# Two projection seams without a wait for the last stores, loads moved into the projections' tails, and a PSUM copy shared with ScalarE

## The chip, the cores and the metric

The kernel runs on one core of a Trainium2 chip. The metric is the device time of one execution, in microseconds. Three runs of the kernel before gave 2546.37, 2546.48 and 2543.38 us (median 2546.37). TensorE (PE) does matmuls and transposes into PSUM, VectorE (DVE) and ScalarE (ACT) do element-wise work and read PSUM, GpSimd (POOL) does element-wise work in SBUF and issues some DMAs, SyncE (SP) issues most DMAs.

## The reference, cut to what matters

A two-layer encoder on 2048 tokens of width 1024, all in float32:

```
h = rms_norm(x, g0); u = h @ w_in_even                   # 2048 x 3328
a = diff_attention(aq, ak, av)       # 4 heads, two maps each, causal by chunks of 64
b = swa_sink_attention(bq, bk, bv)   # 8 heads, window of 128 keys, sinks
x = x + concat(a * silu(ag), b * silu(bg)) @ w_out_even
h = rms_norm(x, g1); u = h @ w_in_odd                    # 2048 x 4096
c = chunk_attention(cq, ck, cv)      # 16 heads, a chunk sees itself and 8 before
x = x + (c * silu(cg)) @ w_out_odd
return rms_norm(x, final_g)
```

## The kernel before, in words

Six stages run one after the other. Each is a block with one program per engine, and between two blocks all five engines meet in a barrier: a stage begins when the last engine has come to the end of its program. In the trace the stages begin about here: first projection 0 us, differential attention 609.0, small (window) attention 978.6, first output 1076.7, second projection 1288, chunk ("band") attention 1964.4, second output 2348.0.

**The projections** (`project`) multiply by one level of Strassen: seven products for a pair of column blocks (a slab, numbered `e`), each of 12 matmuls of 128x128 by 128x512 (high and low parts, L1092). Two passes over the tokens with 13 slabs (first projection) or 16 (second) make `G` slabs; each gives four blocks of 128x512, numbered `n`. The last slab's four blocks are gate blocks in both projections. A gate block goes this way: DVE adds up the products in `full_out` (L945 to L978), ACT makes the sigmoid in `lo_out` (L592), DVE multiplies it into `hi_out` (L868), SP stores it to the DRAM tensor `gt` in two DMAs (L487). `lo_out` and `hi_out` have two buffers each; before ACT writes block `n` it waits until the store of block `n - 2` has landed. At the end SP waits until all stores have landed, and only then does it come to the barrier (L527).

In the last slab POOL already loads operands of the next attention from the DRAM tensors `qh` and `ql` into SBUF that held operands of products that are done (`FirstAhead`, `BandAhead`; POOL waits for the number of finished products, `mm_done`). In the first projection these are the keys of the first 512 tokens after two products, and the queries after six. In the second they are the first 768 columns of four tensors of queries and keys, after four products (L1173). PE waits for them at its first matmul of the attention (`ahead.loaded`).

**The differential attention** begins with 13 DMAs by SP for each further block of 512 tokens, and a small load of the bias by ACT (L1489).

**The band attention** (`band_attn`) goes in 128 steps (8 pairs of heads, 16 token tiles). In each PE makes logits for two heads (L1800), DVE adds the bias and takes the maximum (L1867), ACT exponentiates (L1896), PE turns the result (L1821), DVE and ACT copy it to SBUF, PE multiplies by the values (L1844). PE's logits of step `s + 1` wait for the maxima of step `s`. At the stage's start SP and ACT issue the loads of the columns not yet there and of the values (L1681 to L1685), and POOL loads and masks the bias for the first two heads (L1740 to L1750), then for the next two; DVE's first maximum waits for the first of these (`bias_set`).

**The small attention** (`small_attn`) goes in 32 steps of two tiles and two heads. By step `n`: PE logits (L2043), DVE four maxima into `prob` (L2094), ACT four exponentials (L2130), PE 16 transposes of 64x64 into `turned` (L2057), which lies in two PSUM banks and exists once, DVE one copy of both banks to `prob_t` (L2103), PE the product with the values (L2070). The programs run staggered: PE does logits of step `n`, transposes of `n - 1`, products of `n - 2`; DVE the maxima of `n`, then the copy of `n - 1`. The transposes of a step wait for the copy of the step before. ACT copies the output after every second step (L2137).

## Time and profile before

| what | value |
|---|---|
| runs | 2546.37, 2546.48, 2543.38 us, median 2546.37 |
| profiled execution | 2548.01 us, of which its span is 2546.2 us |
| PE busy | 2369.5 us, 93% of the span |
| DVE, ACT, POOL busy | 1531.6 (60%), 1137.0 (45%), 1071.1 us (42%) |
| mean granted clock of PE | 0.976 of full speed |

The profile lists idle time of an engine with what ended it: another engine, a DMA, or "PEq" where it was PE's own sequencer that came to the instruction late, as it does behind a barrier. PEclk is the clock that was granted to PE, 1.00 for 2.4 GHz and 0.50 for 1.2 GHz.

### The profile page before, as it was taken

Reading aid. Unit: us, or ns where it says so; the run is one execution under the profiler, and the core shown is the slowest. Engines: PE = TensorE matmul, PEld = TensorE weight load, DVE = VectorE, ACT = ScalarE, POOL = GpSimd, SP = SyncE. Lnnn points to the kernel's source line nnn. Section 1 sums busy time; section 2 is a strip of 40 time slices with the busy share of each in tenths; the row PEclk is TensorE's granted clock in tenths of the full one; section 3 lists DMA queues with packets and bytes.
Section 4 is the critical chain, followed back from the end, with each engine's and each line's share of the span. In section 5 each row is a group of like instructions: output and inputs, shape, how many; then the busy total and the mean of one; then the engine's idle time right before and its main releaser. Section 6 shows DMA issues by size and latency. Waiting matters only on the chain. (4 is left out here: it accounts for less than half of the span.)

```text
span 2546.2 us, 46284 instructions
## 1 busy us (share of the span) xinstructions
PE 2369.5 (93%) x17864; PEld 1973.5 (78%) x17864; DVE 1531.6 (60%) x2862; ACT 1137.0 (45%) x2403; POOL 1071.1 (42%) x852
## 2 busy tenths in 40 slices
PE   5999999997999998899879999899997999998998
PEld 4777778875888887688768888788886888887887
DVE  6444565334988897966554423744223888888555
ACT  4333343333777776612143333433332666665221
POOL 6687758773000002310068877678774201100100
PEclk9999999997999999999989999999998999999999
DMA  3555434466663243757334444344433463454452
GB/s 125 173 182 174 157 114 146 145 190 148 138 146 76 62 129 106 219 211 277 130 125 167 157 118 140 116 150 164 141 100 116 159 199 131 148 174 117 163 201 83
DMA packets 220745, 376.76 MB, mean 148 GB/s; under 512 B 54980, under 2 KB 108912, under 8 KB 219504
## 3 DMA queue, kind: packets, MB, share of 16 engines
q1 hardware_dynamic: 199376, 296.21, 36.6%
q0 software_dynamic: 19792, 75.50, 10.0%
q8 instruction: 144, 2.36, 0.4%
q10 hardware_dynamic: 1360, 2.10, 0.3%
q14 instruction: 73, 0.60, 0.1%
HBM read 236.33 MB, written 142.90 MB: 149 GB/s over the span
## 5 line engine op out<-in xcount | busy, mean ns | idle before, releaser
L1092 PE MATMUL p_acc<-p_operands,p_w_hi 128*128 128x512 f32 x1600 | 611.7, 393 | 5.8 <-DVE p_full_out L959 5.5
L310 POOL TENSOR_TENSOR p_w_lo<-p_w_raw,p_w_hi 128x512 fp32r<-128x512 f32 x240 | 333.1, 1396 | 151.3 <-ACT p_w_hi L573 151.0
L1092 PE MATMUL p_acc<-share,p_w_hi 128*128 128x512 f32 x1024 | 385.0, 396 | 12.0 <-DVE p_operands L735 5.6
L1092 PEld LDWEIGHTS p_acc<-p_operands,p_w_hi 128*128 128x128 f32 x1600 | 302.7, 190 | 67.7 <-POOL p_w_raw L328 4.7
L1092 PE MATMUL p_acc<-share,p_w_lo 128*128 128x512 f32 x896 | 350.8, 392 | 0.0
L573 ACT ACTIVATE p_w_hi<-p_w_raw 128x512 fp32r<-128x512 f32 x252 | 156.5, 624 | 245.4 <-POOL p_w_raw L328 106.5
L1092 PE MATMUL p_acc<-share_low,p_w_hi 128*128 128x512 f32 x624 | 249.3, 400 | 12.1 <-DVE p_operands L735 6.1
L1092 PE MATMUL p_acc<-share_low,p_w_lo 128*128 128x512 f32 x624 | 245.2, 393 | 0.0
L1092 PEld LDWEIGHTS p_acc<-share,p_w_hi 128*128 128x128 f32 x1024 | 192.5, 189 | 54.0 <-DVE p_operands L735 8.5
L865 DVE SCALAR_TENSOR_TENSOR p_lo_out<-p_full_out,p_hi_out 128x512 fp32r<-128x512 f32 x116 | 122.5, 1056 | 182.3 <-ACT p_hi_out L590 182.3
L1867 DVE CUSTOM_DVE_ANT_0 c_prob<-c_logits,c_bias 128x640 f32<-128x640 f32 (+4 forms) x256 | 179.5, 739 | 65.6 <-PE c_logits L1800 49.5
L1896 ACT ACTIVATE c_prob<-c_prob,c_neg_max 128x640 f32<-128x640 f32 (+4 forms) x256 | 193.2, 756 | 43.3 <-DVE c_neg_max L1867 43.3
L2354 PE MATMUL o_acc<-w_out_hi,o_m_hi 128*128 128x512 f32 x512 | 203.2, 397 | 3.3 <-DVE o_m_lo L2289 3.3
L2354 PE MATMUL o_acc<-w_out_lo,o_m_hi 128*128 128x512 f32 x512 | 200.9, 392 | 0.0
L2354 PE MATMUL o_acc<-w_out_hi,o_m_lo 128*128 128x512 f32 x512 | 200.7, 392 | 0.0
L1092 PEld LDWEIGHTS p_acc<-share,p_w_lo 128*128 128x128 f32 x896 | 168.7, 188 | 36.0
L1464 ACT ACTIVATE a_prob<-a_prob,a_neg_max 128x128 f32<-128x128 f32 (+15 forms) x128 | 153.5, 1199 | 64.0 <-DVE a_neg_max L1421 63.6
L310 POOL TENSOR_TENSOR p_w_lo<-ready_w,p_w_hi 128x512 fp32r<-128x512 f32 x96 | 132.2, 1385 | 111.5 <-ACT p_w_hi L573 111.5
L1800 PE MATMUL c_logits<-share 64*128 64x256 f32 (+2 forms) x1440 | 138.1, 322 | 30.0 <-DVE c_neg_max L1867 21.4
L945 DVE COPY p_full_out<-p_acc 128x512 f32<-128x512 f32 x56 | 38.7, 691 | 191.8 <-PE p_acc L1092 191.8
L1800 PEld LDWEIGHTS c_logits<-share 64*128 64x128 f32 x1440 | 111.9, 188 | 54.2 <-DVE c_neg_max L1867 38.5
L1844 PE MATMUL c_o<-c_prob_t,c_v 128*64 128x128 f32 x2240 | 151.5, 279 | 0.4 <-issue 0.3
(284 smaller groups left out, 4743.6 us busy)
## 6 DMA issues: line engine op xcount, KB each, us to landing
scr_qh<-p_hi_out SPq DMA_DIRECT2D x116, 256.0 KB, 2.5
scr_ql<-p_lo_out SPq DMA_DIRECT2D x116, 256.0 KB, 2.7
p_w_raw<-in_w_in_even POOLq DMA_DIRECT2D x26, 1024.0 KB, 7.5
scr_gt<-p_hi_out SPq DMA_DIRECT2D x128, 128.0 KB, 2.0
ready_w<-in_w_in_odd POOLq DMA_DIRECT2D x16, 1024.0 KB, 6.9
p_w_raw<-in_w_in_odd POOLq DMA_DIRECT2D x16, 1024.0 KB, 7.0
share<-scr_qh SPq DMA_DIRECT2D x28, 512.0 KB, 8.1
share<-scr_ql SPq DMA_DIRECT2D x28, 512.0 KB, 9.5
```

The lines of the kernel that those rows point to most:

```text
L310: nc.gpsimd.tensor_tensor(w_lo[:, k, :, :], w_source(e, k), w_hi[:, k, :, :].bitcast(F32), ALU.subtract).then_inc(w_made, 1)
L573: nc.scalar.activation(w_hi[:, k, :, :], w_source(e, k), ACT.Copy).then_inc(w_cast, 1)
L865: nc.vector.scalar_tensor_tensor(out=lo_out[:, buf, :], in0=full_out[:, buf, :], scalar=factor, in1=hi_out[:, buf, :].bitcast(F32), op0=AL ...
L945: nc.vector.tensor_copy(full_out[:, n % 2, :], x[:, :]).then_inc(taken, 1)
L1092: last = nc.tensor.matmul(bank[:, :], wt[:, k, c, :], at[k][:, c, :], start=starts and step == 0, stop=step == 3 * HK - 1, skip_group_chec ...
L1464: nc.scalar.activation(p, p, ACT.Exp, bias=neg_max[:, j:j + 1], scale=-1.0, accum_out=row_sum[:, g % 2, m:m + 1]).then_inc(exp_done, 1)
L1800: last = nc.tensor.matmul(logits[half][:, lo:hi], q_sb[b][x][rows, i * P:(i + 1) * P], k_sb[b][y][rows, tile * P:tile * P + hi - lo], star ...
L1844: last = nc.tensor.matmul(o_ps[half * HD:(half + 1) * HD, at:at + P], v, prob_t[:, s % 2, t, half, :], start=t == 0, stop=t == w - 1)
L1867: nc.vector.tensor_tensor_reduce(out=prob[:, j, 0:n], in0=logits[half][:, END - n:END], in1=bias[:, b, WIDE - n:WIDE], scale=1.0, scalar=H ...
L1896: nc.scalar.activation(p, p, ACT.Exp, bias=neg_max[:, j:j + 1], scale=-1.0, accum_out=sums[:, 2 * hp + half, i:i + 1]).then_inc(exp_done, 1)
L2354: last = nc.tensor.matmul(acc[u % 4][:, :], mt[:, t % 2, c, :], wt[:, c, half * BLK:(half + 1) * BLK], start=step == 0, stop=step == 3 * K ...
```

## The change

It has three parts. The code is of the changed kernel where a line has a plus.

**Gates in place.** The last slab's four gate blocks each have a place of their own (`final_place`: two in `lo_out`, two in `hi_out`): ACT writes the sigmoid there, DVE multiplies in place, SP stores it in one DMA that counts on `gates_stored`. ACT's waits for the stores of the last slab itself are gone, and SP's wait at the end covers the slabs before the last only. Those who write to this SBUF in the next stage, or read the gates, wait for `gates_stored`; to make them few, tensors were moved so that only late ones lie there (in the band attention `o_out` and `w_raw`, in the differential attention the small attention's bias).

**Loads in the tail.** Each query of the first projection is loaded as soon as the product that used its place is done (after 3, 4, 5 and 6 products, two DMAs of 128 KB each). In the second projection the four tensors of queries and keys are loaded to half of their columns after 1, 2, 3 and 4 products, then the other half (`rest`); the bias for four heads is loaded after one product into `ahead_place` (which also holds the projection's `x` and `g` buffers) and masked by POOL before the barrier. The band attention's own start is left with the loads of the values, on SP.

**Shared copy.** In the small attention, after every odd step, DVE copies one bank of `turned` and ACT the other; ACT does so between its second and third exponential of the following step.

```diff
...
@@ -123,6 +123,8 @@
+        hi_out = st.sb("hi_out", [P, 2, HT], F32R)
+        lo_out = st.sb("lo_out", [P, 2, HT], F32R)
@@ -281,6 +281,12 @@
+        FINAL = 4 * G - 4
+        def final_place(n):
+            return (lo_out, hi_out)[(n - FINAL) // 2][:, n % 2, :].bitcast(F32)
@@ -411,10 +417,11 @@
-                pool.wait_ge(sem, 16 * 2 * N)
+                pool.wait_ge(sem, 16 * 2 * (N + ahead.BLOCKS))
+            ahead.set_bias(pool)
@@ -482,6 +489,9 @@
+                    if n >= FINAL:
+                        sp.dma_start(gt[at:at + P, first:first + HT], final_place(n)).then_inc(ahead.gates_stored, 16)
+                        return
@@ -524,7 +534,7 @@
-                sp.wait_ge(sem, 16 * 2 * G)
+                sp.wait_ge(sem, 16 * 2 * (G - 1))
@@ -578,7 +588,12 @@
-                if n >= 2:
+                if n >= FINAL + 2:
+                    act.wait_ge(stored_a[buf], 16 * 2 * (G - 1))
+                    act.wait_ge(stored_b[buf], 16 * 2 * (G - 1))
+                elif n >= FINAL:
+                    act.wait_ge(dve_done, seconds[n - 1])
+                elif n >= 2:
@@ -589,7 +604,8 @@
-                    nc.scalar.activation(lo_out[:, buf, :].bitcast(F32), full_out[:, buf, :], ACT.Sigmoid).then_inc(act_done, 1)
+                    to = final_place(n) if n >= FINAL else lo_out[:, buf, :].bitcast(F32)
+                    nc.scalar.activation(to, full_out[:, buf, :], ACT.Sigmoid).then_inc(act_done, 1)
@@ -864,6 +880,8 @@
+                elif n >= FINAL:
+                    nc.vector.tensor_tensor(final_place(n), full_out[:, buf, :], final_place(n), ALU.mult).then_inc(dve_done, 1)
@@ -1132,48 +1150,83 @@
-    def queries(self, eng):
-        for part, near, far in (("qh", slice(0, HD), slice(HD, P)), ("ql", slice(HD, P), slice(0, HD))):
-            self.load(eng, part, 0, near, slice(2, 6, 2))
-            self.load(eng, part, 0, far, slice(3, 6, 2))
+    def query(self, slot):
+        m, s = divmod(slot - 2, 2)
+        rows = (slice(0, HD), slice(HD, P))
+        def load(eng):
+            for x, part in enumerate(("qh", "ql")):
+                row = m * HD
+                eng.dma_start(self.low[rows[(x + s) % 2], slot, 0:BLK].bitcast(F32), self.scr[part][row:row + HD, 0:BLK]).then_inc(self.loaded, 16)
+        return load
-        return [(2, self.keys), (6, self.queries)]
+        return [(2, self.keys)] + [(slot + 1, self.query(slot)) for slot in range(2, 6)]
-    COLS = 3 * NEAR
+    COLS = SEQ // 2
+    BLOCKS = 2 * C_HEADS * HD // SLAB
+    FAR, SET = 3 * P, 3
-    def both(self, eng):
-        for x, part in enumerate(("qh", "ql")):
-            for slot, row in ((x, 0), (2 + x, C_W)):
-                eng.dma_start(self.whole[:, slot, 0:self.COLS].bitcast(F32), self.scr[part][row:row + P, 0:self.COLS]).then_inc(self.loaded, 16)
+        self.place = ctx.enter_context(nc.sbuf_tensor("ahead_place", [P, 3 * D], F32))
+        self.bias = self.place[:, 0:4 * (self.FAR + NEAR)].rearrange("p (h j) -> p h j", h=4)
+    def load_bias(self, pool):
+        pool.dma_start(self.bias[:, :, self.FAR:self.FAR + NEAR], skewed(self.scr["skew_c"], 0, 4)).then_inc(self.bias_loaded, 16)
+    def set_bias(self, pool):
+        nc, bias = self.nc, self.bias
+        nc.gpsimd.memset(bias[:, :, 0:self.FAR], 0.0).then_inc(self.bias_set, 1)
+        pool.wait_ge(self.bias_set, 1)
+        nc.gpsimd.memset(bias[HD:P, :, 0:HD], MASKED).then_inc(self.bias_set, 1)
+        pool.wait_ge(self.bias_loaded, 16)
+        nc.gpsimd.memset(bias[0:HD, :, self.FAR + NEAR - HD:self.FAR + NEAR], MASKED).then_inc(self.bias_set, 1)
+        pool.wait_ge(self.bias_set, self.SET)
+    def one(self, eng, slot, cols, loaded):
+        row = C_W * (slot // 2)
+        eng.dma_start(self.whole[:, slot, cols].bitcast(F32), self.scr[("qh", "ql")[slot % 2]][row:row + P, cols]).then_inc(loaded, 16)
+    def first(self, slot):
+        return lambda eng: self.one(eng, slot, slice(0, self.COLS), self.loaded)
+    def rest(self, eng):
+        for slot in range(4):
+            self.one(eng, slot, slice(self.COLS, SEQ), self.rest_loaded)
-        return [(4, self.both)]
+        return [(1, self.load_bias)] + [(slot + 1, self.first(slot)) for slot in range(4)] + [(4, self.rest)]
...
@@ -1302,6 +1356,7 @@
+            pool.wait_ge(ahead.gates_stored, ahead.GATES)
...
@@ -1621,14 +1676,16 @@
+        o_out = st.sb("o_out", [P, 2, BLK])
-        bias = st.sb("bias", [P, 4, WIDE])
+        bias = ahead.bias
-        o_out = st.sb("o_out", [P, 2, BLK])
...
@@ -1721,40 +1770,25 @@
-            load_bias(0)
-            mask(nc.gpsimd.memset(bias[:, 0:2, 0:WIDE - NEAR], 0.0))
-            mask(nc.gpsimd.memset(bias[HD:P, 0:2, 0:HD], MASKED))
-            finish_bias(0)
-            load_bias(1)
-            mask(nc.gpsimd.memset(bias[:, 2:4, 0:WIDE - NEAR], 0.0))
-            mask(nc.gpsimd.memset(bias[HD:P, 2:4, 0:HD], MASKED))
-            finish_bias(1)
+            pool.wait_ge(first_loaded[-1], 16)
+            pool.wait_ge(ahead.gates_stored, ahead.GATES)
...
@@ -1785,7 +1819,7 @@
-                        pe.wait_ge(first_loaded[-1], 16 * (LOADS + 1))
+                        pe.wait_ge(ahead.rest_loaded, ahead.LOADED)
@@ -1858,8 +1892,10 @@
-                if i == 0 and half == 0:
-                    dve.wait_ge(bias_set, hp + 1)
+                if s == 0 and half == 0:
+                    dve.wait_ge(ahead.bias_set, ahead.SET)
+                if hp >= 2 and i == 0 and half == 0:
+                    dve.wait_ge(bias_set, hp - 1)
@@ -1898,6 +1934,8 @@
+                if n == 0:
+                    act.wait_ge(ahead.gates_stored, ahead.GATES)
@@ -1909,8 +1947,6 @@
-            for n in range(len(FIRST)):
-                first_piece(act, n, 1)
...
@@ -1970,6 +2006,10 @@
+        def shared(n):
+            return n % 2 == 1
@@ -2047,6 +2087,8 @@
+                    if n // 2:
+                        pe.wait_ge(far_copied, n // 2)
@@ -2060,6 +2102,8 @@
+                if shared(n):
+                    pe.wait_ge(far_copied, n // 2 + 1)
@@ -2099,6 +2143,9 @@
+                if shared(n):
+                    nc.vector.tensor_copy(prob_t[:, n % 2, :, 0:HD], turned[:, 0, :].rearrange("p (x q) -> p x q", q=HD)).then_inc(copied, 1)
+                    return
@@ -2120,9 +2167,17 @@
+            def far_leaves(n):
+                act.wait_ge(turned_done, n + 1)
+                if n >= 2:
+                    act.wait_ge(pv_done, n - 1)
+                nc.scalar.activation(prob_t[:, n % 2, :, HD:P], turned[:, 1, :].rearrange("p (x q) -> p x q", q=HD), ACT.Copy).then_inc(far_copied, 1)
+                    if j == 1 and n >= 1 and shared(n - 1):
+                        far_leaves(n - 1)
@@ -2140,6 +2195,7 @@
+                    far_leaves(N - 1)
...
@@ -2304,6 +2360,9 @@
+                if t == 0:
+                    for sem in post.stored:
+                        dve.wait_ge(sem, 16 * (post.heads // 2))
```

The end of SP's program in the first projection, and the beginning of the next stage; before:

```order
246 L487 DMA scr_gt<-p_hi_out 128x256 [waits p0_dve_done]
247 L487 DMA scr_gt<-p_hi_out 128x256
248 L120 UNCONDITIONAL_BRANCH [waits p0_stored_b1,p0_stored_b0,p0_rows_spread,p0_stored_a1,p0_stored_a0]
249 L1264 UNCONDITIONAL_BRANCH [waits barrier_Pool_Activation_PE_DVE_SP_release]
250 L1260 DMA share_low<-scr_qh 64x512
```

and in the changed kernel:

```order
239 L497 DMA scr_gt<-p_hi_out 128x256
240 L493 DMA scr_gt<-p_lo_out 128x512 [waits p0_dve_done] x2
241 L493 DMA scr_gt<-p_hi_out 128x512 [waits p0_dve_done] x2
242 L120 UNCONDITIONAL_BRANCH [waits p0_stored_b1,p0_stored_b0,p0_rows_spread,p0_stored_a1,p0_stored_a0]
243 L1317 UNCONDITIONAL_BRANCH [waits barrier_Pool_Activation_PE_DVE_SP_release]
244 L1313 DMA share_low<-scr_qh 64x512
```

The last four blocks leave in four DMAs of 128x512 instead of eight of 128x256. The wait at the end names the same semaphores, but its count is that of the slab before.

The end of POOL's program in the second projection (up to the branch L120) and its first instructions in the band attention; before:

```order
691 L1173 DMA share<-scr_qh 128x768 [waits p0_rows_stored,p0_rows_spread,p1_mm_done,p0_ident_set,p0_rows_set]
692 L1173 DMA share<-scr_qh 128x768
693 L1173 DMA share<-scr_ql 128x768 x2
694 L120 UNCONDITIONAL_BRANCH
695 L1726 UNCONDITIONAL_BRANCH [waits barrier_Pool_Activation_PE_DVE_SP_gather]
696 L1740 DMA c_bias<-scr_skew_c 128x2x256
697 L1749 MEMSET c_bias 128x2x384
698 L1750 MEMSET c_bias 64x2x64 [waits p0_x_turned]
699 L1745 MEMSET c_bias 64x2x64 [waits p0_split,p0_x_turned]
```

and in the changed kernel (names of semaphores that stages use in turn are those of the first; the last four loads are `rest`):

```order
696 L1206 DMA ahead_place<-scr_skew_c 128x4x256 [waits p0_v_turned,p0_stored_a0,p0_rows_set,p0_stored_a1,p0_stored_b0]
697 L1219 DMA share<-scr_qh 128x1024 [waits p0_rows_set]
698 L1219 DMA share<-scr_ql 128x1024 [waits p0_rows_set]
699 L1219 DMA share<-scr_qh 128x1024 [waits p0_rows_set]
700 L1219 DMA share<-scr_ql 128x1024 [waits p0_rows_set]
701 L1219 DMA share<-scr_qh 128x1024 [waits p0_rows_set]
702 L1219 DMA share<-scr_ql 128x1024
703 L1219 DMA share<-scr_qh 128x1024
704 L1219 DMA share<-scr_ql 128x1024
705 L1210 MEMSET ahead_place 128x4x384
706 L1212 MEMSET ahead_place 64x4x64 [waits ahead_bias_set]
707 L1214 MEMSET ahead_place 64x4x64 [waits ahead_bias_loaded]
```

The bias's load and three memsets have moved from behind the barrier to ahead of it, and eight loads of 512 KB stand where four of 384 KB stood.

ACT in the first steps of the small attention; before:

```order
655 L2121 UNCONDITIONAL_BRANCH [waits barrier_Pool_Activation_PE_DVE_SP_release]
656 L2130 ACTIVATE b_prob,post_sums<-b_prob,b_neg_max 128x128 [waits b_max_done] x2
657 L2130 ACTIVATE b_prob,post_sums<-b_prob,b_neg_max 128x256 [waits b_max_done] x14
658 L2137 ACTIVATE b_o_out<-b_o 128x512 [waits b_pv_done]
659 L2130 ACTIVATE b_prob,post_sums<-b_prob,b_neg_max 128x256 [waits b_max_done] x8
```

and in the changed kernel:

```order
655 L2185 ACTIVATE b_prob,post_sums<-b_prob,b_neg_max 128x128 [waits b_max_done] x2
656 L2185 ACTIVATE b_prob,post_sums<-b_prob,b_neg_max 128x256 [waits b_max_done] x8
657 L2174 ACTIVATE b_prob_t<-b_turned 128x8x64 [waits b_turned_done]
658 L2185 ACTIVATE b_prob,post_sums<-b_prob,b_neg_max 128x256 [waits b_max_done] x6
659 L2192 ACTIVATE b_o_out<-b_o 128x512 [waits b_pv_done]
660 L2185 ACTIVATE b_prob,post_sums<-b_prob,b_neg_max 128x256 [waits b_max_done] x2
661 L2174 ACTIVATE b_prob_t<-b_turned 128x8x64 [waits b_pv_done,b_turned_done]
```

A copy of 128x512 stands between exponentials once in eight of them, that is once in two steps.

## Rows read from the trace of the kernel before

**Rows 1.** Waits of PE over the span: who for whom, us, times, longest.

```profile
PE c_logits L1800 <- DVE c_neg_max L1867: 21.4, 26, 8.1
...
PE a_logits L1325 <- PEq L120: 9.2, 1, 9.2
...
PE c_logits L1800 <- PEq L120: 8.6, 1, 8.6
...
PE a_logits L1325 <- DMA ready_v<-scr_v_a: 5.9, 1, 5.9
```

**Rows 2.** Timeline, first seam: start, duration, engine, line, tiles [idle before, releaser].

```profile
597.43 7.44 SPq L487 DMA_DIRECT2D scr_gt<-p_hi_out  x6
...
599.89 0.69 DVE L978 TENSOR_TENSOR p_full_out<-p_acc,p_near_sum 128x512 f32<-128x512 f32 x1 [0.41 <-PE p_acc L1092]
602.70 0.63 ACT L592 ACTIVATE p_lo_out<-p_full_out 128x512 f32<-128x512 f32 x1 [3.94 <-DMA scr_gt<-p_hi_out]
603.36 0.69 DVE L868 TENSOR_TENSOR p_hi_out<-p_full_out,p_lo_out 128x512 f32<-128x512 f32 x1 [2.78 <-ACT p_lo_out L592]
...
609.04 1.09 PE L1325 MATMUL a_logits<-share_low 128*128 128x128 f32 x4 [9.19 <-PEq L120]
```

**Rows 3.** Waits of SP's queue over the span.

```profile
SPq L527 <- DMA scr_gt<-p_hi_out: 5.1, 2, 3.5
```

**Rows 4.** DMAs issued from 599.4 to 600.0: KB each, us from issue to landing.

```profile
share_low<-scr_ql POOLq DMA_DIRECT2D x1, 256.0 KB, 8.1
```

**Rows 5.** Timeline, second seam.

```profile
1955.46 0.39 PE L1092 MATMUL p_acc<-share,p_w_lo 128*128 128x512 f32 x1
1958.07 0.63 ACT L592 ACTIVATE p_lo_out<-p_full_out 128x512 f32<-128x512 f32 x1 [5.39 <-DMA scr_gt<-p_hi_out]
...
1960.80 0.69 DVE L868 TENSOR_TENSOR p_hi_out<-p_full_out,p_lo_out 128x512 f32<-128x512 f32 x1 [0.78 <-ACT p_lo_out L592]
...
1964.42 0.91 PE L1800 MATMUL c_logits<-share 64*128 64x128 f32 x6 [8.57 <-PEq L120]
...
1965.32 1.28 ACT L1896 ACT_TABLE_LOAD   x1 [4.55 <-PEq L120]
...
1972.59 0.20 POOL L1745 MEMSET c_bias<- 64x128 f32 x1 [6.05 <-DMA c_bias<-scr_skew_c]
1972.82 0.29 DVE L1867 CUSTOM_DVE_ANT_0 c_prob<-c_logits,c_bias 128x128 f32<-128x128 f32 x1 [11.32 <-POOL c_bias L1745]
...
1973.38 0.58 PE L1800 MATMUL c_logits<-share 64*128 64x256 f32 x2 [8.06 <-DVE c_neg_max L1867]
```

**Rows 6.** DMAs issued from 1964.3 to 1964.5: KB each, us from issue to landing.

```profile
c_v<-scr_v SPq DMA_DIRECT2D x1, 128.0 KB, 5.0
```

**Rows 7.** Stretches: busy us (instructions) of PE, PEld, DVE, ACT, POOL; PEclk, DMA share, GB/s.

```profile
1949.00:1956.00 7.00, 6.85 (x31) 5.33 (x29) 3.37 (x5) 0.80 (x2) 1.46 (x3) 1.00 0.87 238
1958.00:1960.00 2.00, 0.00 (x0) 0.00 (x0) 1.27 (x2) 0.63 (x1) 0.00 (x0) 0.55 0.00 0
1982.00:1984.00 2.00, 2.00 (x40) 1.86 (x36) 1.12 (x4) 0.32 (x3) 0.90 (x1) 0.98 1.03 400
```

**Rows 8.** Groups in the small attention, 980 to 1068: busy us, mean ns | idle before.

```profile
L2137 ACT ACTIVATE b_o_out<-b_o 128x512 f32<-128x512 f32 x15 | 8.6, 574 | 0.0
...
L2103 DVE COPY b_prob_t<-b_turned 128x512 f32<-128x512 f32 x4 | 2.7, 683 | 0.0
```

**Rows 9.** Timeline, two steps of the small attention.

```profile
995.76 0.71 PE L2057 MATMUL b_turned<-keep_ident,b_prob 64*128 64x64 f32 x16
...
997.43 0.98 PE L2043 MATMUL b_logits<-share_low 64*128 64x256 f32 x12
...
998.45 0.48 DVE L2094 CUSTOM_DVE_ANT_0 b_prob<-b_logits,ready_bias,keep_sink 128x256 f32<-128x256 f32 x1
...
1000.07 1.22 DVE L2103 COPY b_prob_t<-b_turned 128x1024 f32<-128x1024 f32 x1
...
1001.34 0.71 PE L2057 MATMUL b_turned<-keep_ident,b_prob 64*128 64x64 f32 x16
```

More of the change, by code:

```diff
@@ L140, in project @@
         XS = 4
-        x_sb = st.sb("x", [P, XS if ready is None else 2, D])
+        x_sb = st.sb("x", [P, XS, D]) if ready is None else ahead.place[:, 0:2 * D].rearrange("p (b d) -> p b d", b=2)
         x_buf = [x_sb[:, i, :] for i in range(XS)] if ready is None else [ready.x[:, 0, :], ready.x[:, 1, :], x_sb[:, 0, :], x_sb[:, 1, :]]
-        g_sb = st.sb("g", [P, D])
+        g_sb = st.sb("g", [P, D]) if ready is None else ahead.place[:, 2 * D:3 * D]
         if norm:
@@ L1131 @@
 class FirstAhead:
-    LOADED = 16 * 6
+    LOADED = 16 * 10
+    BLOCKS = 0
     SPARED = 16 * 12
+    GATES = 16 * 4
     def __init__(self, nc, ctx, scr, low):
         self.scr, self.low = scr, low
-        self.loaded = ctx.enter_context(nc.semaphore("first_ahead"))
+        self.loaded, self.gates_stored = (ctx.enter_context(nc.semaphore(f"first_{x}")) for x in ("ahead", "gates_stored"))
     def load(self, eng, part, row, rows, slots):
@@ L1156, in loads @@
     def loads(self):
-        return [(2, self.keys), (6, self.queries)]
+        return [(2, self.keys)] + [(slot + 1, self.query(slot)) for slot in range(2, 6)]
 class BandAhead:
-    COLS = 3 * NEAR
+    COLS = SEQ // 2
     LOADED = 16 * 4
+    BLOCKS = 2 * C_HEADS * HD // SLAB
+    GATES = 16 * 4
+    FAR, SET = 3 * P, 3
     def __init__(self, nc, ctx, scr, whole):
-        self.scr, self.whole = scr, whole
-        self.loaded = ctx.enter_context(nc.semaphore("band_ahead"))
-    def both(self, eng):
-        for x, part in enumerate(("qh", "ql")):
-            for slot, row in ((x, 0), (2 + x, C_W)):
-                eng.dma_start(self.whole[:, slot, 0:self.COLS].bitcast(F32), self.scr[part][row:row + P, 0:self.COLS]).then_inc(self.loaded, 16)
+        self.nc, self.scr, self.whole = nc, scr, whole
+        self.place = ctx.enter_context(nc.sbuf_tensor("ahead_place", [P, 3 * D], F32))
+        self.bias = self.place[:, 0:4 * (self.FAR + NEAR)].rearrange("p (h j) -> p h j", h=4)
+        self.bias_loaded, self.bias_set = (ctx.enter_context(nc.semaphore(f"ahead_{x}")) for x in ("bias_loaded", "bias_set"))
+        self.loaded, self.rest_loaded, self.gates_stored = (ctx.enter_context(nc.semaphore(f"band_{x}")) for x in ("ahead", "rest", "gates_stored"))
@@ L1287, in _ @@
                     sp.wait_ge(pv_done, TILES * (h + 1))
+                    sp.wait_ge(ahead.gates_stored, ahead.GATES)
                     after.load(sp)
@@ L1515, in __init__ @@
         self.nc, self.keep, self.scr, self.share = nc, keep, scr, share
+        self.bias = ctx.enter_context(nc.sbuf_tensor("ready_bias", [P, B_HEADS, NEAR], F32))
         self.v_flat = ctx.enter_context(nc.sbuf_tensor("ready_v", [P, SEQ], F32))
         self.v_sb = self.v_flat[:, :].rearrange("p (h t d) -> p h t d", h=2, d=HD)
-        self.bias = ctx.enter_context(nc.sbuf_tensor("ready_bias", [P, B_HEADS, NEAR], F32))
         self.loaded, self.keys_loaded, self.bias_loaded, self.masked = (
@@ L1645, in band_attn @@
         bias_loaded = st.sems("bias_loaded", 2)
-        bias_masked, bias_set = (st.sem(x) for x in ("bias_masked", "bias_set"))
+        bias_set = st.sem("bias_set")
         qk_done, max_done, exp_done, pv_done, o_done = (
@@ L1675, in values, with first_values @@
             return v_dram[2 * hp:2 * hp + 2].rearrange("h p t d -> p h t d")[:, :, tiles, :]
-        def first_piece(eng, n, x):
-            cols = slice(*FIRST[n])
-            part = scr[("qh", "ql")[x]]
-            if FIRST[n][1] > ahead.COLS:
-                eng.dma_start(q_sb[0][x][:, cols].bitcast(F32), part[q_row:q_row + P, cols]).then_inc(first_loaded[n], 16)
-                eng.dma_start(k_sb[0][x][:, cols].bitcast(F32), part[k_row:k_row + P, cols]).then_inc(first_loaded[n], 16)
-            if x == 0:
-                tiles = slice(FIRST[n][0] // P, FIRST[n][1] // P)
-                eng.dma_start(v_sb[:, 0, :, tiles, :], values(0, tiles)).then_inc(first_loaded[n], 16)
+        def first_values(eng, n):
+            tiles = slice(FIRST[n][0] // P, FIRST[n][1] // P)
+            eng.dma_start(v_sb[:, 0, :, tiles, :], values(0, tiles)).then_inc(first_loaded[n], 16)
         def load_qk(eng, hp, n):
@@ L1723, in _ @@
                         sp.wait_ge(qk_done, TILES * hp)
+                        sp.wait_ge(ahead.gates_stored, ahead.GATES)
                         post.load(sp)
@@ L1834, in pv @@
                     pe.wait_ge(v_loaded[hp % 2][i // (TILES // HALVES)], 16 * loads(hp))
-                if hp == 0 and i < ahead.COLS // P:
+                if hp == 0:
                     for n, (lo, hi) in enumerate(FIRST):
@@ L1951, in small_attn @@
         pair_loaded = [st.sems(f"pair_loaded{b}_", HALVES) for b in range(2)]
-        qk_done, max_done, exp_done, turned_done, copied, pv_done, o_done = (
-            st.sem(x) for x in ("qk_done", "max_done", "exp_done", "turned_done", "copied", "pv_done", "o_done"))
+        qk_done, max_done, exp_done, turned_done, copied, far_copied, pv_done, o_done = (
+            st.sem(x) for x in ("qk_done", "max_done", "exp_done", "turned_done", "copied", "far_copied", "pv_done", "o_done"))
         sink_less, sink_done, summed = (st.sem(x) for x in ("sink_less", "sink_done", "summed"))
```

29 lines of the change are left out of this document (11 added, 18 removed).

## The prediction

> **What bounds the kernel now.** I read the table of busy time first. PE is busy for 93% of the span, so a change that takes no work off PE can only win time in which PE is idle. The view of waits says where that is [rows 1]: apart from many short waits there are two stops behind a barrier (9.2 us ahead of the differential attention, 8.6 ahead of the band attention), and the longest single wait for the maxima of the band attention, 8.1 us, which turns out to be the second half of the same seam. The reader is to see that these come to 26 us and that all three are at places that the change touches.
>
> The timeline of the two seams says what ends last in each. At the first seam [rows 2] DVE has the last block's sum at 599.89 + 0.69 = 600.58, but ACT's sigmoid begins at 602.70, released by the landing of a store of two blocks earlier. DVE's product ends at 604.05, SP has issued the last two stores at 597.43 + 7.44 = 604.87, and waits 3.5 us for them [rows 3]. PE begins at 609.04, 0.65 us after that. At the second seam [rows 5] the last matmul ends at 1955.85. The sigmoid that starts at 1958.07 is of the last block but one; it again waited for a store. The last product ends at 1961.49 and PE begins at 1964.42. It then makes six matmuls and stops until 1973.38: the first maximum needs the bias, and POOL can finish the bias only at 1972.59, after its DMA. In the small attention PE does not stand still for long; there I look at the chain of steps [rows 9].
>
> **The change, part by part.** First seam. ACT no longer waits for a store: sigmoid about 0.1 after the sum, 600.7 to 601.3 (0.63 long), product 601.35 to 602.05 (0.69). SP issues one DMA instead of two; two took 604.87 - 604.05 = 0.8, so one 0.4: 602.45. It does not wait for the landing, and 0.65 us for the barrier gives a start of PE at 603.1. That is 5.9 us earlier. What must be there by then are the queries. Before, 1 MB of them was issued after six products, and the last DMA took 8.1 us to land [rows 4], until about 607.7, hidden under the wait for the stores. Now only 256 KB are issued so late, the rest one, two and three products earlier. If the last two still took 8.1 us from an issue at 598.6, they would land at 606.7 and take 3.6 of the 5.9 back; a DMA that shares the engines with a quarter of the bytes should take well under half of that, so I take nothing for it and keep 3.6 as the bound. The next stage's 13 loads, for which PE waited 5.9 us [rows 1], now start while the last gate store is under way: I take off 0.5. First seam: **5.4 us** (2.3 to 6.5).
>
> Second seam. Both waits for stores go. The last sum can start 0.04 after the last matmul, as it does at the first seam: 1955.9 to 1956.6. Sigmoid to 1957.3, product to 1958.05, one store issued by 1958.45, barrier: PE begins at 1959.1, 5.3 us earlier. The bias is loaded and masked before, so DVE's first maximum follows PE's six matmuls (0.91 us); from there to PE's next logits it took 1973.38 - 1972.82 = 0.56. The second logits then begin at 1959.1 + 0.91 + 0.05 + 0.56 = 1960.6 instead of 1973.38: **12.8 us** in all. The table load of ACT (1.28) starts at the barrier and ends at 1960.4, about when the first exponential needs it. After this the steps are the same.
>
> What could be late here. POOL must be through with its program before the barrier. A product has 12 matmuls, and PE does 31 in 6.85 us [rows 7], so a product takes 2.65 us and the first one of the last slab ends six products before 1955.85, at 1940. From there 0.5 MB of bias and 2 MB of first halves are needed by 1959.1, and the same stretch of the trace moved 238 GB/s: 2.5 MB and two stores of 256 KB take 12.6 us, until 1952.6. With the 2 MB of second halves it is 1961; those are needed only at the ninth step. Should POOL's issue of a load be held up until the bytes before it have moved, it would come to its memsets near 1959, and the seam would give back about 2. The values are now the first DMA of SP in the stage; before, they landed after 5.0 us [rows 6] among the other loads, and 1959.1 + 5 is about when the first step needs them. I take 12.8, with 9 to 15 as bounds.
>
> On this collision the rows show that the store that ACT waited for at the second seam was slow while POOL's loads ran [rows 5, 7]. The Trainium skill (DMA: Bandwidth & Descriptors, section Issuing engines are not separate DMA queues) says that DMAs from ScalarE, SyncE and GpSimd end up on the same 16 engines and interleave. The trace agrees. By that rule 4.5 MB in the tail slow its stores and each other: as long as nobody waits for a late one the sum stays, and if somebody does, the time is that of the second rival below, 2533.3.
>
> Small attention. DVE's copy of 128x512 takes 0.68 where the whole takes 1.22 [rows 8, 9], so 16 steps save DVE 0.54 each, 8.6 us together; that is the upper bound. I take nearly none of it. From transposes to the transposes two steps later it is 5.58 us [rows 9]: transposes, values and logits of PE from 995.76 to 998.41, DVE's four maxima from 998.45 to 1000.07, the copy until 1001.29, and again transposes at 1001.34. The copy in this chain is that of the step between. Where the transposes are of an odd step it is the copy of an even one, which stays whole, so this chain keeps its 5.58 us for two steps; only the other one gets shorter, by 0.54, and there ACT's own copy of 0.57 [rows 8] stands ahead of two of four exponentials. So DVE and PE change one wait for another. The last step is odd and ends 0.54 earlier. **0.5 us** (from 0.5 lost to 8.6 won).
>
> The added waits I cost at nothing. Behind ACT's wait for `gates_stored` in the band attention stand its exponentials, but it comes with the output of the fourth step, and the last store was issued before the stage began; behind those of POOL and SP stand only loads for the output stages. DVE's wait for the attention's stores in the output stage has a whole tile's matmuls ahead of it. If one of them held, it would be for the rest of a landing, some 2 to 4 us.
>
> **Sum.** 5.4 + 12.8 + 0.5 = 18.7 us. The profiled execution took 2548.0, so it would take 2529.3; the median of the runs shown is 1.6 lower, 2546.4, which gives **2527.7**.
>
> **Rivals.** (1) The clock stays up. The granted clock fell to half at 1958.2 (0.55 over 1958 to 1960) and was up again at 1982 [rows 7], so all that the band attention did in its first steps ran at half. If it does not fall in the shorter gap, the 8.6 us from 1973.38 to 1982 could shrink to 4.3 where PE bounds them; DVE and ACT do so in part, so I price it at 3: 2524.7. Against it: it fell 2.35 us after the last matmul, and the new gap is 1959.1 - 1955.85 = 3.2. Chance 0.12.
>
> The Trainium skill (TensorE: Matmul & The Clock Gate, section What's actually happening) says that half rate is the state of an idle array and that activity releases it. The trace agrees that long gaps bring half rate; it shows no gap of 3.2 us. By the rule the time is 2527.7 if such a gap counts as idle, and this rival's 2524.7 if not.
>
> (2) The waits move. Queries late by 3.6 and POOL late by 2 leave 18.7 - 5.6 = 13.1 us: 2533.3. For it: the tail's DMA engines are 87% busy before 3 MB are added [rows 7]. Against it: what is needed first is also issued first. Chance 0.13.
>
> (3) The small attention gets all that DVE saves: 8.6 instead of 0.5, 2519.6. Against it stands the chain of 5.58. Chance 0.03.
>
> (4) Slower: ACT reloads its function table for the copy and again for the next exponential. A table load takes 1.28 [rows 5]; two for each of 16 copies are 41 us, and 2527.7 + 41 = 2568.7. It decides from 0.6 us a copy on, since 16 x 2 x 0.6 = 19. Against it: ACT already copies the output between exponentials every second step, without idle time ahead of it [rows 8]. Chance 0.02.
>
> **How the numbers follow.** The forecast has 0.70: 2523 to 2531 by its own terms. From 2521 to 2536 all but the third and fourth rival and a remainder of misjudged barriers are covered. What differs by less than 0.2%, 5 us, cannot be told from no change. The first three rivals and the forecast are all faster by more; I leave 0.05 for no change (both seams held by something that the profile does not show) and 0.03 for slower.
>
> **What would show it.** After: PE's waits behind the two barriers near 3.2 us each and no wait of 8 us for the band attention's maxima; the last two sigmoids without a DMA as releaser; the second logits 1.5 us after the first; in the small attention two steps still 5.5 to 5.6 apart. It is wrong if PE's wait at a seam names a DMA, or if the small attention gets more than 3 us shorter or longer.

## The result, and the profile after

| | median of the runs | runs | profiled execution | its span |
|---|---|---|---|---|
| before | 2546.43 us (2543.38 to 2547.53) | 4 | 2548.01 us | 2546.2 us |
| after | 2532.53 us (2531.81 to 2536.24) | 4 | 2532.33 us | 2530.5 us |

The ratio is 0.995, with a 95% interval from 0.9933 to 0.9967. The change makes the kernel faster by 13.9 us in the medians and by 15.7 in the two profiled executions; 18.7 were forecast. 2532.5 lies in the range, 4.8 above the predicted time; it lies outside the 2523 to 2531 that the forecast gave its own terms, and next to the second rival's 2533.3. So the direction held, and with it all of the mechanism but one step, and the question is where 3 to 5 us went.

The waits of PE after the change, to be read against [rows 1]:

```profile
PE c_logits L1834 <- DVE c_neg_max L1903: 14.0, 26, 0.7
...
PE a_logits L1380 <- DMA ready_v<-scr_v_a: 6.7, 1, 6.7
...
PE c_logits L1834 <- PEq L120: 6.1, 1, 6.1
...
PE a_logits L1380 <- PEq L120: 3.9, 1, 3.9
```

The 8.1 us for the maxima of the band attention are gone (longest now 0.7). The stop at the first seam fell from 9.2 to 3.9, that at the second only from 8.6 to 6.1. About 3.2 was forecast for each.

The timeline of the first seam answers to [rows 2]:

```profile
598.20 2.90 SPq L493 DMA_DIRECT2D scr_gt<-p_hi_out  x2
598.60 0.69 DVE L996 TENSOR_TENSOR p_full_out<-p_acc,p_near_sum 128x512 f32<-128x512 f32 x1 [0.43 <-PE p_acc L1110]
599.40 0.63 ACT L608 ACTIVATE p_hi_out<-p_full_out 128x512 f32<-128x512 f32 x1 [1.96 <-DVE p_full_out L996]
600.07 0.69 DVE L884 TENSOR_TENSOR p_hi_out<-p_full_out,p_hi_out 128x512 f32<-128x512 f32 x1 [0.78 <-ACT p_hi_out L608]
...
602.43 0.63 PE L1380 MATMUL a_logits<-share_low 128*128 128x128 f32 x4 [3.87 <-PEq L120]
...
605.31 1.01 PE L1380 MATMUL a_logits<-share_low 128*128 128x256 f32 x3 [2.25 <-DVE a_neg_max L1476]
```

The sigmoid's releaser is DVE's sum and no longer a DMA. SP has issued the last store at 601.10, and PE begins 1.33 later; before, PE began 0.65 after SP's wait was over.

The second seam answers to [rows 5]:

```profile
1944.55 0.53 POOL L1219 DMA_DIRECT2D share<-scr_ql  x1
...
1946.89 0.31 POOL L1214 MEMSET ahead_place<- 64x256 f32 x1
...
1949.96 2.90 SPq L493 DMA_DIRECT2D scr_gt<-p_hi_out  x2
...
1951.83 0.69 DVE L884 TENSOR_TENSOR p_hi_out<-p_full_out,p_hi_out 128x512 f32<-128x512 f32 x1 [0.78 <-ACT p_hi_out L608]
1956.34 1.40 SPq L1734 DMA_DIRECT2D c_v<-scr_v  x3
...
1956.38 0.91 PE L1834 MATMUL c_logits<-share 64*128 64x128 f32 x6 [6.06 <-PEq L120]
...
1957.43 0.29 DVE L1903 CUSTOM_DVE_ANT_0 c_prob<-c_logits,ahead_place 128x128 f32<-128x128 f32 x1 [4.91 <-PE c_logits L1834]
...
1958.00 1.01 PE L1834 MATMUL c_logits<-share 64*128 64x256 f32 x6 [0.71 <-DVE c_neg_max L1903]
```

POOL's memsets are through at 1947.20, DVE's product at 1952.52, SP's last store is issued at 1952.86, and yet all engines start only at 1956.3. The rows of the line that ends a projection (L120) for this stretch say who was missing. The columns are the shortest, median and longest duration in ns, and the first and last start in us:

```profile
L120 POOLq DRAIN  x1: 8705/8705/8705, 1947.4 to 1947.4; - x1
L120 ACTq DRAIN  x1: 639/639/639, 1951.2 to 1951.2; - x1
L120 DVEq DRAIN  x1: 725/725/725, 1951.8 to 1951.8; - x1
...
L120 SPq DRAIN  x1: 7/7/7, 1953.2 to 1953.2; - x1
```

A block ends with a drain on every engine. ACT's and DVE's last as long as their last instruction; SP's takes 7 ns, although its store is still under way. POOL's takes 8.7 us, until 1956.10, 2.9 after SP's. POOL's own last load, by the DMA view of its issue, landed 11.0 us after 1944.55, that is at 1955.55:

```profile
share<-scr_ql POOLq DMA_DIRECT2D x1, 512.0 KB, 11.0
```

Theory D therefore says: at the end of a block POOL's drain lasts until POOL's own DMAs have landed, and the loads that were moved into the tail hold the barrier. The rivals: the barrier waits for something else (R), or PE misses the data and not the barrier (L).

### The profile page after: what moved, and what is told of

Same layout as the page of the kernel before. It is cut to its first block and busy times, and to the rows that moved or that the text cites. A ratio compares the mean times of both kernels' runs of the same rounds, so it can differ in the third digit from the quotient of the medians.

```text
span 2530.5 us, 46330 instructions
## 1 busy us (share of the span) xinstructions
PE 2365.2 (93%) x17864; PEld 1971.4 (78%) x17864; DVE 1521.6 (60%) x2862; ACT 1145.2 (45%) x2419; POOL 1074.1 (42%) x856
## 5 line engine op out<-in xcount | busy, mean ns | idle before, releaser
L1903 DVE CUSTOM_DVE_ANT_0 c_prob<-c_logits,ahead_place 128x640 f32<-128x640 f32 (+4 forms) x256 | 179.5, 738 | 60.0 <-PE c_logits L1834 55.3
L1110 PEld LDWEIGHTS p_acc<-share_low,p_w_hi 128*128 128x128 f32 x624 | 118.2, 189 | 40.3 <-DVE p_operands L751 8.5
```

Of the source, the lines that this page charges most:

```text
L1110: last = nc.tensor.matmul(bank[:, :], wt[:, k, c, :], at[k][:, c, :], start=starts and step == 0, stop=step == 3 * HK - 1, skip_group_chec ...
L1903: nc.vector.tensor_tensor_reduce(out=prob[:, j, 0:n], in0=logits[half][:, END - n:END], in1=bias[:, b, WIDE - n:WIDE], scale=1.0, scalar=H ...
```

## The experiments

All kernels are the changed one with the edit shown. Times are medians; the kernel before took 2548.2, 2548.2 and 2547.9 us beside the three groups.

**The change once more, twice.**

> The changed kernel once more, for how much the stages of one program differ from one profile to the next. Theory D (at the end of a projection POOL does not reach the barrier before its own DMAs have landed): both seams as before, PE starts the band attention about 6 us after its last matmul, 3 us after SP has issued the last store; 2532.5 us. If the rest of the miss is scatter, the stages without an edit (projections up to their last matmul, output stages) differ from the first profile by up to 1.5 us; if it is a cost of the change, they agree within 0.3.

2533.0 us (2527.4 to 2536.1). PE's stop at the second seam was 3.7 here and not the 6 us expected; the drain took 6.39 us and ended 0.6 after SP's:

```profile
L120 POOLq DRAIN  x1: 6394/6394/6394, 1945.2 to 1945.2; - x1
...
L120 SPq DRAIN  x1: 7/7/7, 1951.1 to 1951.1; - x1
```

> The changed kernel a third time, beside the version with the second halves loaded behind the barrier. Theory D: PE's idle time at the second seam is 3.7 to 6.1 us, by when POOL's own loads have landed (6.06, 5.86, 6.14 and 3.74 in the profiles so far of kernels with all second halves on POOL's queue). The projection from its first transpose to its last matmul takes 682 to 683 us, or 688 where the granted clock was 0.50 for longer at its short stops.

2529.5 us (2527.1 to 2533.9), the stop 3.9 us. So the same 4.5 MB held the barrier 2.9 us in one execution and 0.6 and 0.8 in two. The landing of POOL's last load moved with it: 8.7 us after its issue in the first control, 11.0 in the first profile.

**POOL's drain left out, at the end of the two projections.**

```diff
-        block = ctx.enter_context(nc.Block())
+        block = ctx.enter_context(nc.Block(no_gpsimd_drain=True))
```

> The changed kernel, but POOL's drain instruction at the end of the two projections is left out; every load and every semaphore stays. Theory D (the drain lasts until POOL's own loads have landed, and is what comes last at the barrier): in the first profile SP was through at 1953.2 and POOL's drain at 1956.1, at the first seam at 601.5 and 602.15; so PE starts 2.9 and 0.65 earlier, 3.5 in all: 2529.0 us, PE's waits behind the barriers 3.2 each. Rival R (the barrier waits for something else, a store in flight or the change of program itself): nothing moves, 2532.5. Rival L (PE needs the data and not the barrier): PE starts as early, but its first matmuls then wait for a load as long as the drain did, 2532.5, with a DMA as releaser.

PE's stops are as theory D has them, and against R and L. No wait on a DMA came in their place at these starts.

```profile
PE a_logits L1380 <- PEq L120: 3.3, 1, 3.3
PE c_logits L1834 <- PEq L120: 3.2, 1, 3.2
```

The time was 2534.7 us (2529.2 to 2536.7), not 2529.0. The stops were shorter and the profiled execution was not. The stretch that took it back, the second projection, is told below; the kernel with late queries and without the drain does not show it.

**The second halves behind the barrier.**

```diff
-        return [(1, self.load_bias)] + [(slot + 1, self.first(slot)) for slot in range(4)] + [(4, self.rest)]
+        return [(1, self.load_bias)] + [(slot + 1, self.first(slot)) for slot in range(4)]
...
                 first_values(sp, n)
+            ahead.rest(sp)
```

> The changed kernel, but the second halves of the queries and keys (2 MB) are loaded by SP at the start of the band attention, behind its three loads of values. Theory D: POOL's queue holds 2.5 MB instead of 4.5; 2 MB at the 400 GB/s of that stretch are 5 us, so its drain ends near 1951, ahead of SP's 1953.2; PE starts 2.9 us earlier and needs the second halves only at the ninth step, 20 us later: 2529.6 us. Rival R (the barrier is held by something else): 2532.5. Rival C (the loads at the start of the stage are what is short there): the values come later and the start gains up to 2.9 and loses 2 or more, 2531.6 or above, with PE waiting for a DMA.

2530.3 us (2527.6 to 2534.1). POOL's drain is through at 1951.6, five us before SP's, PE's stop is 3.2 us, and no wait on the values came in its place:

```profile
L120 POOLq DRAIN  x1: 2941/2941/2941, 1948.6 to 1948.6; - x1
...
L120 SPq DRAIN  x1: 7/7/7, 1956.5 to 1956.5; - x1
...
  PE c_logits L1835: 3.2, 1
```

> The second halves loaded by SP behind the barrier, once more. Theory D: PE's idle time at the second seam is 3.15 again, since POOL's drain is through before SP, so 0.6 to 2.9 us less than the control of this call; the median of all executions 1 to 3 us lower. If the lower median of the first time (2530.3 against 2533.0) was scatter, the idle time is lower and the medians agree within 1 us.

2529.3 us (2527.4 to 2530.4), the stop 3.15 again. By all executions the median of this version is 2530.3 (10), that of the change 2532.4 (14, 2527.1 to 2536.2). Its median is the lowest of all versions, 2 us below the change, but in the last group it was level with the control (2529.3 and 2529.5); the shorter stop is shown, the shorter time only likely.

**The last loads by SP, in flight at the barrier.** SP issues the second halves (first seam: the last query) between the second and the third gate store.

```diff
                     store(n)
+                    if n == FINAL + 1:
+                        for free, load in ahead.late_loads():
...
+                            load(sp)
```

> The changed kernel, but SP issues the last loads of both tails, between the second and the third gate store: the second halves (2 MB) at the second seam, the last query (256 KB) at the first. They are in flight at the barrier as before, only on SP's queue. Theory D (only POOL's own DMAs hold POOL): PE starts 2.9 and 0.65 earlier, the third store goes out 0.3 late, the last one in time: 2529.0 us. A barrier that waits for any DMA in flight would start PE later than now, since the second halves are issued 4 us later: about 2536. Rival R: 2532.5.

2532.9 us. SP's last load is issued at 1948.28, later than POOL's were in the first profile, and POOL's drain takes 3.2 us and SP's 7 ns: a DMA in flight on SP's queue holds no barrier. The stops are 3.2 and 3.3. But the values, which SP issues behind these 2 MB, come late, and PE waits for them in the first steps:

```profile
PE c_o L1891 <- DMA c_v<-scr_v: 4.3, 1, 4.3
PE c_logits L1847 <- PEq L120: 3.2, 1, 3.2
```

That is the collision that the prediction weighed, on SP's queue instead of POOL's, and it takes back more than the stop gave: what PE needs first must also be issued first.

**The queries late, with and without the drain.**

```diff
-        return [(2, self.keys)] + [(slot + 1, self.query(slot)) for slot in range(2, 6)]
+        return [(2, self.keys), (6, self.queries)]
```

> The changed kernel, but the first projection loads all queries after six products, in four DMAs of 256 KB, as the kernel before did; the gates stay in place, so SP no longer waits for stores. Theory D (POOL's drain comes last at the barrier): in the kernel before that drain ended 8.3 us after the last matmul, hidden behind SP's wait for stores; it comes into the open now. PE starts 8.5 us after its last matmul instead of 3.9, and ACT, SP and POOL start the next stage as late as PE: about 4.6 us longer than the control, 2537.6 us. Rival L (only PE's own wait for the queries): the other engines start at 3.9, PE's first matmul names a DMA and starts at 6.9, when they have landed: 2536. Rival S (the prediction's sum: the last two loads take well under half of 8.1 us and hold nobody): PE at 3.9, 2533.

2537.6 us, as theory D had it. ACT, SP and PE start together, 9.0 us after the last matmul, though SP waits for no store:

```profile
606.08 0.36 ACTq L1549 DMA_DIRECT2D a_bias<-scr_skew_a  x1
606.08 0.31 POOL L1353 MEMSET a_bias<- 128x256 f32 x1 [8.96 <-POOLq L120]
606.08 0.52 SPq L1318 DMA_DIRECT2D share_low<-scr_qh  x1
...
606.12 1.09 PE L1385 MATMUL a_logits<-share_low 128*128 128x128 f32 x4 [8.96 <-PEq L120]
```

> The kernel with the late queries, and without POOL's drain at the end of the two projections. Theory D: all engines but PE start 3.2 us after the last matmul; PE waits for the queries themselves until about 6.9, with a DMA as releaser; at the second seam PE starts at 3.2. If the drain were not what holds the stage, nothing changes against the kernel with the late queries (PE and the others at 8.5, or all at 3.9).

2535.5 us. The others start at 3.2, and only PE waits, with a DMA named:

```profile
602.13 0.35 ACTq L1549 DMA_DIRECT2D a_bias<-scr_skew_a  x1
...
608.86 1.11 PE L1385 MATMUL a_logits<-share_low 128*128 128x128 f32 x4 [9.97 <-DMA share_low<-scr_ql]
```

PE waits 3 us longer than forecast: POOL's last load landed 9.9 us after the last matmul, against 7.9 in the kernel with the drain. SP's 13 loads now run beside it, which is the likely reason and was not tested. From the last matmul to the small attention it is still 2.0 us shorter than with the drain (376.1 against 378.1).

At the second seam this gives a simple table; times count from the end of the last matmul:

| kernel | SP's drain done | POOL's drain done | PE starts |
|---|---|---|---|
| the change, three profiles | 2.9 | 5.8, 3.5, 3.7 | 6.1, 3.7, 3.9 |
| queries late | 2.9 | 5.6 | 5.9 |
| second halves behind, two profiles | 2.9 | -2.1, -1.7 | 3.15, 3.15 |
| last loads by SP | 2.9 | -1.8 | 3.2 |
| no drain, early and late queries | 2.9 | none | 3.2, 3.2 |
| bias behind, copy not shared (both below) | 2.9, 2.9 | 3.7, 5.9 | 4.0, 6.1 |

PE starts 0.26 to 0.29 after the later of the two. Without POOL's drain it is 0.33 after SP's. Leaving it out also changes how the engines report at the barrier: PE, ACT, DVE and SP show two semaphore instructions there instead of one. The argument does not hang on that kernel alone, since the second halves behind the barrier and the last loads by SP keep POOL's drain and bring the same short stop.

The Trainium skill (PSUM — Partial Sum Buffer, section Engine vs sequencer instructions) says that a drain waits for the engine to go fully idle. The trace agrees for ACT and DVE; it adds that POOL's drain counts POOL's DMAs in, and that SP's does not count SP's.

**The bias behind the barrier.**

```diff
-            ahead.set_bias(pool)
...
+            ahead.load_bias(pool)
+            ahead.set_bias(pool)
             st.clear_before(pool)
```

> The changed kernel, but POOL loads and masks the band attention's bias for four heads behind the barrier, as its first work of the stage; all other loads stay in the tail. Theory P (the prediction's second half of the second seam, 7.5 us): POOL issues the bias 0.4 after PE's start and has it masked after 8.2, as before the change, so PE's second logits come 9 us after its start instead of 1.6: 7.4 us longer than the control, 2540.4. Rival Q (the bias was late only because of the loads of 6 MB that started with it, which are now in the tail): it lands after 4.6 us as it does in the tail now, the second logits come 5.5 us after the start, 3.9 longer: 2536.9.

2537.4 us. POOL masked the bias 6.9 us after PE's start (1954.22), between P and Q:

```profile
1954.62 0.76 POOL L1205 DMA_DIRECT2D ahead_place<-scr_skew_c  x1 [9.61 <-POOLq L120]
...
1960.79 0.30 POOL L1213 MEMSET ahead_place<- 64x256 f32 x1 [3.66 <-DMA ahead_place<-scr_skew_c]
1961.13 0.29 DVE L1904 CUSTOM_DVE_ANT_0 c_prob<-c_logits,ahead_place 128x128 f32<-128x128 f32 x1 [8.66 <-POOL ahead_place L1213]
```

The second logits came 7.5 us after PE's start instead of 1.3 to 1.6, so the early bias is worth 6 of the 7.5 us that the prediction gave it. Loaded behind the barrier it is ready 1.5 us sooner than before the change (8.4 after PE's start, [rows 5]), with fewer loads issued beside it.

**The copy not shared.** `shared(n)` returns False, and the waits for ACT's copy are left out.

> The changed kernel, but DVE copies both banks in every step of the small attention and ACT none. Theory C (the chain of two steps keeps the whole copy of the even step): two steps 5.5 to 5.6 us apart in both kernels, the stage from PE's first logits to the output stage's first matmul 98.1 us instead of 97.4; 0.5 to 0.8 us longer than the control, which its time can't tell. Rival F (the stage follows DVE's busy time, 16 x 0.54): 8.6 us longer, 106 us for the stage, 2541.6.

2531.2 us (2527.1 to 2531.7), no longer than the controls. The stage took 97.7 us, where 98.1 were expected; with the shared copy it was 97.4, 97.4 and 97.3 in the three profiles of the change. Nothing came of the sharing that can be measured. Where DVE's saving went is seen in DVE's maxima over 80 us of the small attention (busy us, mean ns | idle before), before the change and after it:

```profile
L2094 DVE CUSTOM_DVE_ANT_0 b_prob<-b_logits,ready_bias,keep_sink 128x256 f32<-128x256 f32 (+1 forms) x116 | 48.3, 473 | 0.6 <-PE b_logits L2043 0.6
```

```profile
L2138 DVE CUSTOM_DVE_ANT_0 b_prob<-b_logits,ready_bias,keep_sink 128x256 f32<-128x256 f32 (+1 forms) x116 | 48.3, 472 | 8.5 <-PE b_logits L2083 8.5
```

DVE's idle time ahead of them rose from 0.6 to 8.5 us; in the kernel with the whole copy it is 0.6 again. DVE waits for PE, whose two steps are as far apart as in [rows 9]:

```profile
988.40 0.71 PE L2099 MATMUL b_turned<-keep_ident,b_prob 64*128 64x64 f32 x16 [0.32 <-DVE b_prob_t L2150]
...
992.72 1.22 DVE L2150 COPY b_prob_t<-b_turned 128x1024 f32<-128x1024 f32 x1
...
993.99 0.71 PE L2099 MATMUL b_turned<-keep_ident,b_prob 64*128 64x64 f32 x16 [0.35 <-DVE b_prob_t L2150]
```

## Why the prediction was right in kind and too large

Stretches in us, between first instructions of PE or its last matmul (the last one to the end of the span), in the profile of before and in the first profile and the two controls of the change; "forecast" and "gain" (before less first) are what the stretch loses. PE's first instruction of the second projection, a transpose, comes at 1274.4 us before the change; 1288 is where its first product begins.

| stretch | before | first | controls | forecast | gain |
|---|---|---|---|---|---|
| first projection to its last matmul | 587.8 | 586.5 | 586.2, 584.6 | 0 | 1.3 |
| first seam, to the second logits | 12.0 | 6.8 | 6.6, 6.5 | 5.4 | 5.2 |
| rest of the differential attention | 366.8 | 365.9 | 365.5, 366.0 | 0 | 0.9 |
| small attention | 98.1 | 97.4 | 97.4, 97.3 | 0.5 | 0.7 |
| first output | 197.7 | 198.6 | 198.1, 198.5 | 0 | -0.9 |
| second projection to its last matmul | 681.4 | 683.1 | 682.5, 683.2 | 0 | -1.7 |
| second seam, to the second logits | 17.5 | 7.7 | 5.0, 5.2 | 12.8 | 9.9 |
| rest of the band attention | 374.7 | 375.5 | 375.4, 376.5 | 0 | -0.8 |
| second output | 198.1 | 197.1 | 197.0, 197.9 | 0 | 1.0 |

- **Second seam: the step that failed.** The store waits and the wait for the bias went as forecast. The step "POOL must be through with its program before the barrier" followed POOL to its memsets, which were through at 1947.2, and stopped there. POOL's drain behind them was missed, and it cost 2.9 us in the first profile and 0.6 and 0.8 in the controls: the term of 12.8 measured 9.9, 12.5 and 12.3. The time of landing itself had been worked out well: 1961 for the second halves, 5.2 us after the last matmul, against 5.2 in the first profile and 2.9 and 3.1 in the controls. What failed was to let them land off the path because PE needs them only at the ninth step. The sign that was set for this, a DMA named by PE's wait at a seam, did not come either: the wait names PE's sequencer, and the DMA stands one step further back, behind POOL's drain. The second rival gave POOL's lateness 2 us, close in size but by another cause. The drain stood in the trace of before as well, at 9.45 and 8.38 us; there SP's wait for the stores ended 0.6 and 6.2 later and hid it:

```profile
L120 POOLq DRAIN  x1: 9452/9452/9452, 598.7 to 598.7; - x1
...
L120 SPq DRAIN  x1: 7/7/7, 608.8 to 608.8; - x1
...
L120 POOLq DRAIN  x1: 8376/8376/8376, 1949.6 to 1949.6; - x1
...
L120 SPq DRAIN  x1: 7/7/7, 1964.2 to 1964.2; - x1
```

- **First seam: near its number, in part by luck.** PE began 3.9 us after its last matmul and not at the 3.25 of the sum, because the drain ended 0.65 after SP's there too:

```profile
L120 POOLq DRAIN  x1: 5611/5611/5611, 596.5 to 596.5; - x1
...
L120 SPq DRAIN  x1: 7/7/7, 601.5 to 601.5; - x1
```

  Against this, the 0.5 taken off for the 13 loads did not show before the second logits. PE's wait for `ready_v` grew from 5.9 to 6.7, but it lies in the next stretch, which did not get longer. The two about cancel, and 5.4 measured 5.2. The last query's load took 4.5 us, more than the "well under half" of 8.1 that the prediction took; no wait of PE names it, but the drain did wait for it. That the start was not later still is due to the spread queries. Had only the store waits been removed, the late queries would have kept the start at 9.0 through the drain, and nearly the whole 5.9 would have been lost: the bound of 3.6 for late queries was too kind.
- **Small attention: right in its reason.** The chain kept its two steps, and DVE's saving became idle time. The number is chance: the kernel without the sharing is 0.5 shorter than before too, so 0.3 or 0.4 of the 0.7 at most is the sharing's, which is within the scatter of other stretches. The third and fourth rivals did not come about; ACT loads a table once in the stage, as before.
- **The clock rival**: half rate came at the second seam in all profiles of changed kernels, with stops of 3.15 to 6.1 us. Two stretches of the first profile (columns as in [rows 7]):

```profile
1956.00:1966.00 10.00, 7.97 (x74) 6.75 (x74) 4.68 (x19) 5.24 (x15) 0.91 (x1) 0.53 0.83 273
1966.00:1976.00 10.00, 9.44 (x152) 8.28 (x152) 8.91 (x16) 7.07 (x19) 3.99 (x3) 1.00 1.03 377
```

  Counted from the second logits the clock was back after about 8 us (1958.0 to 1966), before the change after 8.6 (1973.4 to 1982). So the rival's condition did not come about, and from the second logits on the stage took as long as before (375.5 against 374.7). The prediction was wrong that the trace before shows no gap of 3.2 us. It has one of 3.3 us that ends at 1333.1 and one of 3.1 that ends at 1601.5, and half rate followed the first but not the second (columns as in [rows 7]):

```profile
1334.00:1337.00 3.00, 3.00 (x8) 2.33 (x8) 0.00 (x0) 0.00 (x0) 2.84 (x3) 0.51 0.89 302
...
1602.00:1606.00 4.00, 4.00 (x20) 3.26 (x19) 3.62 (x4) 0.98 (x2) 3.21 (x3) 1.00 0.20 66
```

- **The rest of the 4.8** lies between executions and in the stretches forecast at 0, which differ by up to 1.9 us between the three profiles of the change. About 1.5 of it is the runs of before that the sum started from: over all 35 executions that kernel's median is 2547.9 and not 2546.4, which makes the gain 15.5. The second projection lost 0.8 us against before between 331 and 380 us after its start in each of three profiles (the first, a control, the last loads by SP), and 0.4 in that of the copy not shared; what costs it was not tried.

One more thing made medians hard to compare: the second projection took 682.0 to 683.2 us to its last matmul in nine profiles of changed kernels and 687.8 and 688.1 in two (without the drain, and the first with the second halves behind). These two stretches of 4 us are from a control and from the kernel without the drain, each about 3 us behind the end of the same stop of 3.1 us (columns as above):

```profile
1596.00:1600.00 4.00, 4.00 (x24) 3.39 (x23) 3.22 (x5) 1.78 (x3) 2.42 (x3) 1.00 0.20 66
```

```profile
1600.00:1604.00 4.00, 4.00 (x12) 3.17 (x11) 3.22 (x5) 1.78 (x3) 2.40 (x3) 0.60 0.20 66
```

The same DVE and ACT work runs in both, but PE makes 24 matmuls at 2.4 GHz in the one, and 12 in the other with most of the stretch at 1.2 GHz. In the faster execution the clock did not fall there. This stop accounts for about half of the 5.3 us between the two; the rest had been lost before it, part of it behind two earlier stops, where half rate lasted longer too. The profiled execution of the kernel without the drain (2534.7) is also its median, so this is how a kernel with a shorter seam can come out 1.7 us above its control; for its other executions, which have no trace, it is not shown.

## What to carry to other kernels

Where stages meet in a barrier, look at what each engine's last instruction there waits for, drains included, and count the loads in flight on GpSimd's queue as its work: here a load moved ahead of the barrier on that queue held it until it had landed, and one issued by SyncE did not. Prefetch on GpSimd only what lands before the other engines are through, and issue the rest behind the barrier, after what is needed first. When a wait is removed, the next one may already stand in the old trace, hidden by less than a microsecond.

## What the runs showed that was not expected

- POOL's drain ended 0.3 to 1.0 us after the landing of POOL's last load at all 20 seams that have one (1951.58 after 1951.21, 1956.10 after 1955.55, 602.15 after 601.20); SP's took 7 ns with 2 MB in flight on its queue.
- The same 4.5 MB in the tail landed 8.7 or 11.0 us after the last issue in executions of one program. Why was not found.
- Stops of about 3 us inside a projection brought half rate in some executions, and none or less of it in others; the projection took 5 us longer in two of eleven profiles, about half of it behind one such stop.
